# Output-weight sums made early in a DRAM scratch by GpSimd's transfers, and the output projection's 28 blocks loaded plainly

## The reference

```python
sh, sc, gt = adaln(c, w_ada[l], b_ada[l])
h_l = rmsnorm(x_l, norm_g[l]) * (1.0 + sc) + sh          # 512 x 2048
u_l = h_l @ w_in[l]                                       # the input projection
...
out_l = mixer(u_l, keys_all, lp, rope, True)              # long convolution | attention | pooling
x_l = x_l + gt * (out_l @ w_out[l])                       # the output projection, 512x2048 by 2048x2048
return rmsnorm(x_l, final_norm_g)
```

## Time and profile before

| | |
|---|---|
| Median of 3 runs | 968.86 us (968.47 to 969.57) |
| Profiled execution: its own time | 970.46 us |
| Profiled execution: span in the profile | 968.6 us |
| PE busy | 902.9 us (93%) |
| DVE, ACT, POOL busy | 683.6, 426.7, 191.6 us |
| Bytes read and written in HBM | 152.22 MB, 4.19 MB |

### The profile page before, as it was taken

One profiled execution on the slowest core, in us unless ns is written; L12 is line 12 of the kernel. 1 busy time (PEld: TensorE's weight loads), 2 busy tenths in 40 slices (PEclk: granted clock), 3 DMA queues, 4 the chain that ended last, 5 costly groups with the idle time before them and its releaser, 6 DMA issues.

```text
span 968.6 us, 12203 instructions
## 1 busy us (share of the span) xinstructions
PE 902.9 (93%) x4754; PEld 746.6 (77%) x4754; DVE 683.6 (71%) x857; ACT 426.7 (44%) x633; POOL 191.6 (20%) x153
## 2 busy tenths in 40 slices
PE   9999999999999999999999999999999896968475
PEld 6777788888888888888888898989988675756364
DVE  5545997789976998579747667878787465634455
ACT  4655574444444434332334254545454452432253
POOL 2221202200031000010067300000121213222971
PEclk9999999999999999999999999999999898998888
DMA  9999822232332222788723312100114889399433
GB/s 359 419 419 420 353 95 93 76 98 88 108 99 66 66 87 87 257 300 309 259 87 114 137 66 66 44 23 2 55 44 159 227 191 308 74 249 267 131 136 124
DMA packets 34213, 158.91 MB, mean 164 GB/s; under 512 B 3915, under 2 KB 5323, under 8 KB 25324
## 3 DMA queue, kind: packets, MB, share of 16 engines
q1 hardware_dynamic: 31376, 140.70, 39.4%
q0 software_dynamic: 2304, 16.78, 9.0%
q10 hardware_dynamic: 476, 0.66, 0.2%
HBM read 152.22 MB, written 4.19 MB: 161 GB/s over the span
## 4 chain that ended last, share of the span: by engine, by line
PE 72%; DMA 13%; DVE 6%; ACT 4%; POOL 2%; issue 2%; SPq 0%; ACTq 0%; POOLq 0%; DVEq 0%
PE pp L2361 38%; PE pp L2391 15%; DMA wo_sum<-in_w_out_dram 7%; PE pp L2671 5%; PE pp L2276 4%; DMA ada_raw<-in_w_ada_dram 3%; DMA wo_raw<-in_w_out_dram 3%; DVE wo_lo L1921 2%; PE pp L2252 2%; ACT wo_hi L1214 2%; PE pp L2637 2%; PE pp L2282 1%; PE pp L2629 1%; PE pp L2628 1%; DVE softmax_stats L1882 1%
## 5 line engine op out<-in xcount | busy, mean ns | idle before, releaser
L2361 PE MATMUL pp<-h_hi,w_hi 128*128 128x512 f32 x544 | 213.0, 391 | 0.0
L2361 PE MATMUL pp<-h_hi,w_lo 128*128 128x512 f32 x544 | 211.9, 389 | 0.0
L2361 PE MATMUL pp<-h_lo,w_hi 128*128 128x512 f32 x544 | 211.8, 389 | 0.0
L2671 PE MATMUL pp<-wo_hi,side_hi 128*128 128x512 f32 x224 | 94.9, 424 | 48.9 <-DVE wo_lo L1921 33.0
L1597 DVE TENSOR_TENSOR w_lo<-w_raw,w_hi 128x1024 fp32r<-128x1024 f32 x68 | 87.6, 1288 | 66.3 <-ACT w_hi L957 65.5
L957 ACT ACTIVATE w_hi<-w_raw 128x1024 fp32r<-128x1024 f32 x68 | 71.8, 1056 | 129.4 <-PE pp L2361 121.1
L2361 PEld LDWEIGHTS pp<-h_hi,w_lo 128*128 128x128 f32 x544 | 102.1, 188 | 21.5
L2361 PEld LDWEIGHTS pp<-h_hi,w_hi 128*128 128x128 f32 x544 | 102.2, 188 | 21.2 <-DVE w_lo L1597 0.3
L2361 PEld LDWEIGHTS pp<-h_lo,w_hi 128*128 128x128 f32 x544 | 102.2, 188 | 20.5
L2671 PEld LDWEIGHTS pp<-wo_hi,side_hi 128*128 128x128 f32 x224 | 45.1, 202 | 65.3 <-DVE wo_lo L1921 37.4
L2671 PE MATMUL pp<-wo_lo,side_hi 128*128 128x512 f32 x224 | 92.1, 411 | 0.0
(11 more groups left out here) (371 smaller groups left out, 1962.8 us busy)
## 6 DMA issues: line engine op xcount, KB each, us to landing
w_raw<-in_wb_dram SPq DMA_DIRECT2D x68, 512.0 KB, 3.8
ada_raw<-in_w_ada_dram SPq DMA_DIRECT2D x15, 2048.0 KB, 13.3
w_gate_raw<-in_w_gate_dram SPq DMA_DIRECT2D x16, 1024.0 KB, 6.5
wo_sum<-in_w_out_dram POOLq DMA_DIRECT2D x16, 1024.0 KB, 9.4
wo_raw<-in_w_out_dram SPq DMA_DIRECT2D x12, 1024.0 KB, 6.2
wo_sum<-in_w_out_dram SPq DMA_DIRECT2D x8, 1024.0 KB, 8.5
wa_raw<-in_wa_dram SPq DMA_DIRECT2D x14, 288.0 KB, 7.9
UG<-in_xT_dram SPq DMA_DIRECT2D x7, 512.0 KB, 8.7
```

Of the source, the lines that this page charges most:

```text
L2361: mm = eng.matmul(ps[i][:], w, x, start=(kk == 0 and m == 0), stop=(kk == KT - 1 and m == 2))
L2671: mm = eng.matmul(ps[BANKS[u][b] + tok][:], a, v[:, w:w + L], start=u in (1, 7, 6) and c == 0 and k == 0 and m == 0, stop=c == 1 and k == ...
```

## The change

- A DRAM scratch `w_sums` of 16 blocks (1 MB each) is added. GpSimd's transfers fill it during the input projection: after the filters' first sums, the four blocks of 5 and of 7 are copied from `w_out` (DRAM to DRAM) and one more quarter is added to each by accumulating transfers; after the filters' second sums, the sums of 7 are copied as the start of 6 and a quarter is added; between the two norm sums the sums of 6 are copied as the start of 4, and after the second norm sum a quarter is added.
- In the output projection all 28 blocks are loaded plainly by SP, in order, into four places (`N_RAW`); there are no more `load_sum` and `add_weights`. SP issues the load of block n when PE has finished block n-4.
- There are three places for high halves (`N_HIGH`): block n's high half waits for PE to finish block n-3.
- `y_right` moves to the place of the sides of product 7; the loads of `x` (`y_left`, `y_right`) and of the gain are put between block loads.
- GpSimd multiplies the held products by the gate in a function of its own (`gated`); ACT's and DVE's lists around the blocks are put in a new order (holds, row squares and finished blocks one or two blocks later, and ahead of the block's low half on DVE).

```diff
+SUMS = (5, 7, 6, 4)
+N_RAW, N_HIGH = 4, 3
...
-        wo_places = (FREE, FREE + 5, 29)
+        wo_places = (FREE, FREE + 5, FREE + 10, FREE + 21)
...
-        wo_high_ = [at("wo_hi0", 19, 2048, F32R), at("wo_hi1", FREE + 16, 2048, F32R)]
-        wo_sum = [at(f"wo_sum{i}", p, 2048) for i, p in enumerate((FREE + 21, FREE + 10, TAB, TAB + 4))]
+        wo_high_ = [at("wo_hi0", 19, 2048, F32R), at("wo_hi1", FREE + 16, 2048, F32R), at("wo_hi2", 29, 2048, F32R)]
+        w_sums = nc.dram_tensor("w_out_sums", [16, P, 2048], F32, kind="Internal").ap()
...
+        def w_sum(u, b, c):
+            return w_sums[4 * SUMS.index(u) + 2 * b + c, :, :]
...
             def load_out(n):
                 u, b, c = CHUNKS[n]
-                if n >= 3:
-                    eng.wait_ge(wo_mm, n - 2)
-                eng.dma_start(wo_raw[n % 3][:], w_out(u != 1, u == 3, b, c)).then_inc(wo_in[n % 3], 16)
+                if n >= N_RAW:
+                    eng.wait_ge(wo_mm, n - N_RAW + 1)
+                if u in SUMS:
+                    eng.wait_ge(sum_in[SUMS.index(u)], 128)
+                    src = w_sum(u, b, c)
+                else:
+                    src = w_out(u != 1, u == 3, b, c)
+                eng.dma_start(wo_raw[n % N_RAW][:], src).then_inc(wo_in[n % N_RAW], 16)
...
             eng.wait_ge(s_mm, 32)
-            load_sum(4)
-            eng.wait_ge(pool_mm, 4)
             load_out(2)
-            load_sum(5)
             load_out(3)
...
+            for n in range(4, 28):
                 load_out(n)
+                if n == 6:
+                    eng.wait_ge(pv_mm, 8)
+                if n in (6, 7):
+                    for i in (2 * n - 12, 2 * n - 11):
+                        eng.dma_start(y_left[:, 2 * i * L:2 * (i + 1) * L], t["x"][i * P:(i + 1) * P, 0:1024]).then_inc(y_in[0], 16)
...
+            def copied(u, part):
+                side, half = part
+                for b, c in itertools.product(range(2), repeat=2):
+                    eng.dma_start(w_sum(u, b, c), w_out(side, half, b, c)).then_inc(sum_in[SUMS.index(u)], 16)
+
+            def begun_with(u, other):
+                eng.wait_ge(sum_in[SUMS.index(other)], 128)
+                for b, c in itertools.product(range(2), repeat=2):
+                    eng.dma_start(w_sum(u, b, c), w_sum(other, b, c)).then_inc(sum_in[SUMS.index(u)], 16)
+
+            def added(u, part):
+                side, half = part
+                eng.wait_ge(sum_in[SUMS.index(u)], 64)
+                for b, c in itertools.product(range(2), repeat=2):
+                    eng.dma_start(w_sum(u, b, c), w_out(side, half, b, c), accum_op=ALU.add, max_dma_last_dim=8192).then_inc(sum_in[SUMS.index(u)], 16)
...
+                if o == 0:
+                    copied(5, (0, 0))
+                    copied(7, (0, 1))
+                    added(5, (0, 1))
+                    added(7, (1, 1))
+                else:
+                    begun_with(6, 7)
+                    added(6, (0, 0))
...
             for i, x in enumerate((prob(0), q_square(0))):
+                if i:
+                    begun_with(4, 6)
...
+            added(4, (1, 0))
...
             def wo_high(n):
...
-                if n >= 2:
-                    eng.wait_ge(wo_mm, n - 1)
+                eng.wait_ge(wo_in[n % N_RAW], WO_FROM[n % N_RAW] + 16 * (n // N_RAW) + 16)
+                if n >= N_HIGH:
+                    eng.wait_ge(wo_mm, n - N_HIGH + 1)
```

More of the change, by code:

```diff
@@ L8 @@
+import itertools
 import math
@@ L432, in backbone @@
         held, held6, side_made = sem("product_held"), sem("part6_held"), sem("side_made")
[L435 to L438, removed]
+        y_in, gain_in, wo_in = x_in[0:2], x_in[2], (*ada_in, wb_in[0])
+        WO_FROM = (*(16 * len(range(s, KT + 1, 3)) for s in range(3)), 16 * len(range(0, 4 * B_GROUPS, KW)))
+        sum_in = [sem(f"weight_sum{u}_in") for u in SUMS]
         mix_hi, mix_lo, gate_out = sem("mix_hi"), sem("mix_lo"), sem("gate_out")
@@ L624, in _ @@
             eng.wait_ge(s_mm, 32)
-            load_sum(4)
-            eng.wait_ge(pool_mm, 4)
             load_out(2)
-            load_sum(5)
             load_out(3)
[L630 to L651, removed]
-                load_out(n)
+            for n in range(4, 28):
+                load_out(n)
+                if n == 6:
[3 more added lines that the diff above has]
+                        eng.dma_start(y_left[:, 2 * i * L:2 * (i + 1) * L], t["x"][i * P:(i + 1) * P, 0:1024]).then_inc(y_in[0], 16)
+                if n == 9:
+                    eng.wait_ge(side_made, 6)
+                    eng.wait_ge(mix_lo, 8)
+                    eng.dma_start(gain, t["gain"].to_broadcast([P, D]).rearrange("p (k c) -> p k c", c=256)).then_inc(gain_in, 16)
+                if n in (19, 20):
+                    if n == 19:
+                        eng.wait_ge(wo_mm, chunk_of(7, 1, 1) + 1)
+                    for i in (2 * n - 38, 2 * n - 37):
+                        eng.dma_start(y_right[:, 2 * i * L:2 * (i + 1) * L], t["x"][i * P:(i + 1) * P, 1024:D]).then_inc(y_in[1], 16)
             for i, tok in enumerate(LAST_TOKENS):
@@ L776, in gains, with gated @@
                     eng.tensor_tensor(y, y, gain[:, 2 * b:2 * b + 2, :], ALU.mult).then_inc(gained, 1)
-            def subtract_ahead(b):
[L780 to L784, removed]
+            def gated(b):
+                g = gate_rows_[:, (2 + b) * L:(3 + b) * L]
+                eng.wait_ge(gate_out, 1)
+                eng.wait_ge(held6, 2 * b + 2)
+                eng.wait_ge(held, 2 * b + 6)
+                for x in (*product1[b], *product7[b]):
+                    link(eng.tensor_tensor(x[:], x[:], g, ALU.mult))
+            def subtract_ahead(b):
                 for i in range(2):
@@ L804, in _ @@
             side(6, 1)
-            for u in (6, 4):
-                for c in range(2):
-                    add_weights(chunk_of(u, 0, c))
             for c in range(2):
-                add_weights(chunk_of(7, 1, c))
                 side(3, c)
+            gated(0)
             eng.wait_ge(gain_in, 32 + 16)
[L812 to L820, removed]
+            gains((2, 0), (3, 0), (0, 0), (1, 0), (0, 1), (1, 1))
             eng.wait_ge(y_in[1], 32 + 64)
-            eng.wait_ge(held, 8)
-            add_weights(chunk_of(5, 1, 0))
             subtract_ahead(0)
-            add_weights(chunk_of(5, 1, 1))
+            gated(1)
             subtract_ahead(1)
@@ L1388, in _ @@
             side_high(7, 0)
+            side_high(7, 1)
+            wo_high(4)
             hold(1, 0)
-            wo_high(4)
-            side_high(7, 1)
+            wo_high(5)
             hold(1, 1)
-            wo_high(5)
             side_high(6, 0)
@@ L1416, in _ @@
                     row_squares(1, 1)
-                if n == 16:
+                if n == 17:
+                    side_high(5, 1)
+                if n == 18:
                     hold(7, 1)
-                    side_high(5, 1)
-                if n == 20:
+                if n == 22:
                     side_high(3, 0)
-                if n == 21:
                     row_squares(2, 1)
                     row_squares(3, 1)
+                if n == 23:
                     side_high(3, 1)
-                if n == 23:
+                if n == 24:
                     row_squares(2, 2)
                     row_squares(3, 2)
-                if n == 25:
+                if n == 26:
                     for tok in range(2, 4):
                         row_squares(tok, 3)
-                    for i in range(2):
-                        last_root(i)
-                        last_scale(i)
-                if n == 27:
-                    row_squares(0, 2)
-                    row_squares(1, 2)
+            for i in range(2):
+                last_root(i)
+                last_scale(i)
+            row_squares(0, 2)
+            row_squares(1, 2)
             for i in range(2, 4):
```

85 lines of the change are left out of this document (29 added, 56 removed).

## The result

The changed kernel takes 952.83 us (median of 4 runs, 952.44 to 953.73) against 968.66 us (4 runs, 967.17 to 969.57): a ratio of 0.9839, interval 0.9822 to 0.9856. It is 15.8 us faster, where 34 us were forecast; 952.8 us lies in the range. The profiled execution took 952.44 us with a span of 950.6 us (before 970.46 and 968.6), so its spans differ by 18.0 us.

The account below looks back on a forecast made before the run. PE was taken as the bound until about 750 us, then waiting for weights in the output projection. 970.5 - 58 (output projection) + 24 (input projection) = 936.5 us, 935 as median; range 911 to 968 us.

Parts of the forecast that it names:

- What it puts into the input projection: Input projection: 16 copies and 16 additions on GpSimd's queue delay PE's chunk loads, costing 24 us with the clock.
- Output projection, 58 us: Output projection: plain block loads make PE the bound, 139.0 us in place of 199.8; gain 58 us, bounds 45 to 61.
- POOL's subtractions ... eight operations ... are 11 us: Output projection: after `y_right` loads behind block 15, eight operations at 1.3 to 1.4 us fit in six blocks, 33 us.
- Price of a copy, 2.84 us: Input projection: a 1 MB DRAM to DRAM copy takes all engines as long as a plain load, 2.84 us; upper bound 5.45.
- The rival of slow DRAM to DRAM transfers: Input projection: slow copies or slow DRAM altogether starve PE, up to 1017 us; chance 0.19 for 966 to 1017 us.
- Price of an addition, 5.45 us: Input projection: adding 1 MB to a sum in DRAM takes 5.45 us as in SBUF, at most 8.3 us.
- The queues take turns by piece, and a copy's piece is 64 KB: Input projection: a chunk's load waits one piece each turn, up to 24 us beside copies, 6.9 us beside additions.
- The rival of copies that don't hinder: Input projection: copies cost PE nothing, only the additions' 2 + 3 us are lost, 916 us; chance 0.24.
- The copies' loss, 19 us with the clock: Input projection: the forecast loss of 24 us less the additions' 5 us, including lower clock after two long stalls.
- The first group: Input projection, 8 copies from about 184.6 us, then 8 additions: a 7.9 us stall and about 2 us, 10 us together.
- The additions' loss, 5 us: Input projection: about 2 us beside the first group's 8 additions, 0 in the second, 3 us in the fourth.
- Clock, 2.3 us for each long stall, 4.6 us in all: Input projection: each of two long stalls brings PE to the lower clock level for one chunk, 2.3 us each.

Follow-up runs that it names:

- e1: The changed kernel without any copy or addition of the sums, blocks loading one plain quarter in place of a sum: 909.94 us, ratio 0.9379 to the kernel before.
- e2: The changed kernel with the 16 copies kept in place and the 16 additions left out: 932.92 us, ratio 0.9625 to the kernel before.
- e3: The changed kernel with the copies cut into 8 KB pieces as the additions are, nothing left out: 930.76 us, ratio 0.9591 to the kernel before.
- e4: The changed kernel with copies and additions cut into 4 KB pieces: 920.21 us, ratio 0.9485 to the kernel before.
- e8: The changed kernel with pieces capped at 2 KB, taken by the additions only (copies stayed at 4 KB): 916.65 us, ratio 0.9449 to the kernel before.
- e5: The changed kernel with copies in 8 KB pieces and the inverse tables' load (`inv_raw`) issued four chunks earlier: 930.47 us, ratio 0.9594 to the kernel before.

## Why the prediction was right or wrong

The direction and the range were right, and so was the mechanism, turns between two queues; the size was not. The step that failed is "What it puts into the input projection", the term of 24 us, which measured 42.4; within it, above all, the additions, put at 5 us, which measured 20.2.

- **Output projection, 58 us.** Right: 60.4 us between the spans and 60.6 by e1. Each block takes 5.49 us, where 5.56 were read from two blocks in the earlier trace rows, and no block waits for its load. Two errors of about the same size stood in it unseen: the stretch before really ended at 959.8 us and not at 957.1, so that 65.2 us were won; and the close is 4.8 us longer. "POOL's subtractions ... eight operations ... are 11 us" failed: POOL has 22 operations from `y_right`'s landing on, and they take 2.2 us and not 1.3 in the mean. The price was taken from the input projection, though the trace of before held operations of the output projection with up to 3.4 us. And POOL waits for the whole of `y_right`, whose last part goes out one block later than was written, after block 16. At the end the chain runs through POOL; that this sets the longer close is read from the chain and from DVE's wait, and no run here tested it alone.
- **Price of a copy, 2.84 us.** Right: 2.97 us (e2). The rival of slow DRAM to DRAM transfers falls. The 214 GB/s that the Trainium skill gives (DMA: Bandwidth & Descriptors, section "Latency and other measured facts") are exceeded here: 353 GB/s each way.
- **Price of an addition, 5.45 us.** Right, with the sum in DRAM as well: 5.17 us.
- **The queues take turns by piece, and a copy's piece is 64 KB.** Shown: the packets of the two queues alternate in the trace (e2, e3), and cutting the pieces alone gives back 22, 33 and 36 us of 43 (e3, e4, e8). The load that was to land at 208.6 us lands at 209.2 (e2), and the stall of 7.9 us measures 8.79, partly by luck: "8 x 3.02 = 24 us" has one packet in a turn beside a copy, and the trace has two, after a start 5.3 us late. The rival of copies that don't hinder falls with it. The Trainium skill (DMA: Bandwidth & Descriptors, section "Queues, rings and completion order") has an engine change queues only at a packet's end, which the traces bear out (SP's packets moved only in bursts between the 64 KB pieces), and gives some 9 to 17 descriptors for a packet, which they don't: then a copy cut in eight pieces per engine would have held an engine as long as an uncut one, and e3 would have cost what the change costs.
- **The copies' loss, 19 us with the clock** (the 24 less the additions' 5). Nearly right: 22.2 us (e2). The first group gave 12.1 for 10.2, the third 7.5 for 8.3; the second cost 2.6 us in place of nothing.
- **The additions' loss, 5 us** ("8 additions last 8 chunk loads of 6.9 us, chunks here come every 6.7: about 2 us"; fourth group 3 us). This failed: 20.2 us (42.4 - 22.2), of which 12.0 in the first group, 1.7 in the second, 3.5 in the fourth, and 3.0 in the third, where no addition runs and the copies only fall otherwise against the chunks. The price of a turn was right: beside additions the loads of a full queue landed 6.2 us apart. Three things were put at nothing.

  The first is what the copies leave behind: the chunks' loads stood in SP's queue with no room to catch up. The second is two more loads in that queue, of `inv_raw` and `w3`; the prediction counted chunk loads alone. SP's transfers of the changed kernel:

```profile
195.09 0.42 SPq L545 DMA_DIRECT2D inv_raw<-in_tables_dram  x1
...
239.82 0.33 SPq L522 DMA_DIRECT2D w_raw<-in_w_dram  x1
242.57 14.11 SPq L516 DMA_DIRECT2D w_raw<-in_wb_dram  x3
```

  Issue and time to landing give the landings: 218.0 us, 223.6 (`inv_raw`), 229.9, 236.1, 242.3, 249.9 (`w3`), 256.1 us. Both are 128 rows, so each asks 8 turns of every engine, as many as a chunk; `inv_raw`, with half a chunk's bytes, took 5.6 us of the queue. The loss steps up at just these places: DVE's low half is 14.7 us late before `inv_raw` (14.5 in e2), 18.8 us behind it (13.2), and 25.1 us behind `w3` (13.2).

  The third is a late start, in every group. A chunk's load with nothing beside it starts to move 0.97 us after its issue (23 loads of this trace). Beside additions it was 3.4 and 3.6 us for the two that were issued at 342.82 and 533.05 us with no load ahead of them, and they took 10.06 and 10.10 us to land where 6.9 were worked out; beside copies it was 5.3 and 5.5 us (188.20 and 327.70 us). So even without `w3` the load of 242.57 us would have landed at an estimated 252.7 us and not at 249.5; `w3` accounts for 3.4 us of its delay. Smaller pieces do not remove this: 3.5 us beside the 2 KB pieces of e8. What makes the start late no run here shows, and how the 12.0 us divide between the three was not tested: no run took `w3` out, and e5 moved `inv_raw` where no backlog stood.

  The fourth group came out at 3.5 us for 3, by another way than was written: not four loads each 1.4 us short, but one wait of 3.2 us for ACT, behind a load of 10.1 us.
- **What is queued behind the waiting instruction.** The prediction named what PE waits for and left out ACT's list: behind a late high half stands the evacuation of products that PE needs sooner than the weights, with a table load of 1.28 us before it in one case (259.22 us) and three casts, 2.3 us, in the other (554.88 us). In the profile after 6.1 of 32.0 us of PE's waits have this form (3.2 + 2.9), in e3 8.0 of 12.1 us.
- **Clock, 2.3 us for each long stall, 4.6 us in all.** Right in kind: half chunks of 4.61 us at 232.32 and of 4.58 at 259.22 us, where half chunks of e2 took 2.75 to 3.02. But the clock fell to its lower level behind five of the stalls and not two. PE worked 17 us at that level between 205 and 475 us, an estimated 8.7 us lost; with the 32.0 us of waits that is 40.7 of the 42.4 us.
- **HBM bytes**: 25 MB more read and 33.6 written, where 42 and 34 were forecast. The prediction counted 40 blocks; there are 60 (28 loads, 16 copies, 16 additions) in place of 36 (12, 8, 16), so 24 more.

## What to carry to other kernels

When a background transfer shares the DMA engines with loads that an engine waits for, its price is the turn and not the bytes: count the turns, add the late start (0.97 us became 3.4 to 5.5 us here), and cut the pieces (copies in 4 KB and additions in 2 KB cost 36 us less than 64 and 8 KB, with the engines no less full). Look up the pieces in the trace afterwards, since a cap need not be taken as it is written. Count all transfers in the queue of the waiting loads, small tables too, since each takes as many turns as it has packets; where the balance is within a few per cent, one more transfer is a stall. Moving the background elsewhere only helps if no short transfer there stands in everyone's way: the attention's 2 us swap took 19.28 us.

## What was not expected of the hardware

- A transfer from DRAM to DRAM ran at 353 GB/s in each direction, an accumulating one in DRAM at no more than in SBUF (5.17 us for 1 MB against 5.45).
- Small pieces cost the engines little: 141 us for the sums in e8 (15.4% of 914.6 us) in place of 130 us (13.7% of 950.6 us), with a quarter of the size for the additions and a sixteenth for the copies (4 KB; the cap of 2 KB was not taken for them).
- A load whose queue was empty started to move 3.4 to 3.6 us after its issue beside additions and 5.3 to 5.5 us beside 64 KB copies, 0.97 us with nothing beside it.
- Beside 64 KB pieces two packets of 4 KB passed in a turn; beside pieces of 8 KB it was one for one.
- POOL's subtractions on 128x512 took between 1.25 and 3.31 us in the same stretch (884.74 to 894 us), with operands of the same shape; what decides it was not tested.
